# One encoder layer on one core: the gates' stores ahead of a large load, four reorderings, and the last tile pair's sums made by TensorE

## The reference

```python
def _swiglu(x, w_gate, w_up, w_down):
    return (jax.nn.silu(x @ w_gate) * (x @ w_up)) @ w_down

h = x
h = h + FFN_RES * _swiglu(_rmsnorm(h, ffn1_norm), ffn1_w_gate, ffn1_w_up, ffn1_w_down)   # FFN_RES = 0.5, D_FF = 2816
n = _rmsnorm(h, mix_norm)
z = n @ w_in                       # -> c_q 256 | c_kv 128 | k_rope 32 | u 512 | g_attn 1024 | g_ssm 1024
attn = ...                         # 8 heads, low-rank q and kv, rotary part of 32
y_ssm = ...                        # complex diagonal recurrence, forward and backward, plus ssm_d * u
glu = jax.nn.gelu(y_ssm) @ w_glu + b_glu
ssm_out = glu[..., :SSM_WIDTH] * jax.nn.sigmoid(glu[..., SSM_WIDTH:])
merged = (jax.nn.sigmoid(g_attn) * (attn @ w_o_attn) + jax.nn.sigmoid(g_ssm) * (ssm_out @ w_o_ssm))
h = h + merged @ w_out
h = h + FFN_RES * _swiglu(_rmsnorm(h, ffn2_norm), ffn2_w_gate, ffn2_w_up, ffn2_w_down)
out = _rmsnorm(h, final_norm)
```

## Time and profile before

| | |
|---|---|
| runs | 2243.97, 2243.58, 2242.82 us |
| median of the three | 2243.58 us |
| profiled execution | 2243.45 us |
| its span, first to last instruction | 2241.4 us |
| PE busy | 2140.1 us, 95% of the span |
| DVE, ACT, POOL busy | 66%, 41%, 27% |
| mean granted TensorE clock | 0.987 |

### The profile page before, as it was taken

How to read it: one execution, slowest core, us unless ns; L and a number is a source line. 1 busy time by engine, 2 the same in 40 slices (tenths; PEclk the granted TensorE clock), 3 DMA queues, 4 the chain that set the end, 5 groups by cost and what they waited for, 6 DMA issues and landing times. The chain is left out here.

```text
span 2241.4 us, 27668 instructions
## 1 busy us (share of the span) xinstructions
PE 2140.1 (95%) x10074; PEld 1770.1 (79%) x10074; DVE 1468.3 (66%) x2294; ACT 917.6 (41%) x1550; POOL 611.3 (27%) x510
## 2 busy tenths in 40 slices
PE   6999999999999998999999999899899999999997
PEld 4778888887887896787777887788688888887886
DVE  7787667657777527961557887554865656657777
ACT  5423323324445433124427778423523232324444
POOL 5336877740000012220002333100633333310000
PEclk9999999999999999999999999999999999999999
DMA  3434334349332545331440000274133232349333
GB/s 124 107 91 127 118 118 130 122 167 339 111 99 97 184 76 141 100 94 47 124 141 16 7 7 15 88 264 155 46 105 113 85 117 83 120 161 346 98 99 109
DMA packets 234583, 263.00 MB, mean 117 GB/s; under 512 B 34832, under 2 KB 169488, under 8 KB 233936
## 3 DMA queue, kind: packets, MB, share of 16 engines
q1 hardware_dynamic: 234448, 261.23, 36.7%
HBM read 184.60 MB, written 76.58 MB: 117 GB/s over the span
## 5 line engine op out<-in xcount | busy, mean ns | idle before, releaser
L48 PE MATMUL psum<-f_B_hi,f_A_hi 128*128 128x512 f32 x1232 | 487.5, 396 | 21.9 <-DVE f_A_lo L1048 10.1
L50 PE MATMUL psum<-f_B_hi,f_A_lo 128*128 128x512 f32 x1232 | 482.3, 392 | 0.0
L49 PE MATMUL psum<-f_B_lo,f_A_hi 128*128 128x512 f32 x1232 | 482.2, 391 | 0.0
L48 PEld LDWEIGHTS psum<-f_B_hi,f_A_hi 128*128 128x128 f32 x1232 | 232.9, 189 | 73.6 <-DVE f_A_lo L1048 17.1
L50 PEld LDWEIGHTS psum<-f_B_hi,f_A_lo 128*128 128x128 f32 x1232 | 232.8, 189 | 49.3
L49 PEld LDWEIGHTS psum<-f_B_lo,f_A_hi 128*128 128x128 f32 x1232 | 233.1, 189 | 47.3
L938 ACT CAST f_A_hi<-f_S 128x512 fp32r<-128x512 f32 x176 | 109.3, 622 | 347.0 <-PE psum L50 339.6
L48 PE MATMUL psum<-f_wd,f_hh 128*128 128x512 f32 x616 | 240.6, 391 | 3.6 <-DVE f_wd L1094 3.6
L49 PE MATMUL psum<-f_wd,f_hh 128*128 128x512 f32 x616 | 240.3, 390 | 0.0
L50 PE MATMUL psum<-f_wd,f_hh 128*128 128x512 f32 x616 | 240.2, 390 | 0.0
L1318 POOL TENSOR_TENSOR f_S<-f_raw 128x512 f32<-128x512 f32 x86 | 129.0, 1500 | 300.9 <-DVE f_A_lo L1048 280.3
(11 more groups left out here) (336 smaller groups left out, 4179.2 us busy)
## 6 DMA issues: line engine op xcount, KB each, us to landing
f_h_raw<-hidden SPq DMA_DIRECT2D x154, 256.0 KB, 2.7
hidden<-rows SPq DMA_DIRECT2D x44, 768.0 KB, 4.5
f_raw<-ffn_w_gate SPq DMA_DIRECT2D x44, 512.0 KB, 5.2
f_raw<-ffn_w_up SPq DMA_DIRECT2D x44, 512.0 KB, 5.0
f_wd_raw<-ffn_w_down SPq DMA_DIRECT2D x44, 512.0 KB, 9.2
rows<-x SPq DMA_DIRECT2D x16, 512.0 KB, 7.0
ga_raw<-w_in SPq DMA_DIRECT2D x16, 512.0 KB, 4.4
gates<-ga_sig SPq DMA_DIRECT2D x32, 256.0 KB, 2.4
```

The lines of the kernel that those rows point to most:

```text
L48: pe.matmul(out, lhs_hi, rhs_hi, start=first, stop=False, skip_group_check=go_on)
L49: pe.matmul(out, lhs_hi, rhs_lo, start=False, stop=False, skip_group_check=go_on)
L50: return pe.matmul(out, lhs_lo, rhs_hi, start=False, stop=last, skip_group_check=go_on)
```

## The change

Six things are changed; line numbers of the code before stand in brackets.

1. In both FFN fronts the sums of the last tile pair are no longer made by POOL and turned. `turn_last_sums` writes them into the banks as products of the normalised rows (stationary, plain f32) with the identity or with a new tile `minus` = -identity, which ACT makes once: 4 x (1 + 2 + 2 + 3 + 4) = 48 products of 128 columns in place of 20 transposes.
2. Between the last matrix and the units DVE's parts for unit 2 stand between the second and the third `pair_sum` (they stood behind the first weight difference).
3. In the last group of units each `final_row` stands one unit earlier. At the end of the second FFN `final_var(2)` stands ahead of `final_row(5)`, and the last row is scaled and stored in two halves.
4. The square of row 2 moves from the end of the first FFN to the start of the projection. There DVE makes the lo parts of turns 0 to 3 and `rp.low(0)` ahead of the norm's inverse root, and PE makes turn 4 behind the first product instead of ahead of it, so that each later turn moves back by one product.
5. In the SSM phase the load of `C_mat` is cut into four of 1024 KB, issued ahead of the stores of gates 2 to 5; the stores of gates 0 and 1 and the load for gate 4 come ahead of them.
6. In the mixer the two lo parts of keys move from n = 1 to n = 3 and n = 4.

```diff
     def act(self, act, rp):
         rest = slice(0, ST - self.AHEAD)
+        self.act_square(act, ST - self.AHEAD - 2)
         self.act_square(act, ST - self.AHEAD - 1)
...
-        dve.wait_ge(self.s_sq, 1)
+        dve.wait_ge(self.s_sq, 2)
         dve.tensor_scalar(st[:, 1, rest], st[:, 0, rest], 1.0 / D, EPS, ALU.mult, ALU.add).then_inc(self.s_var, 1)
-        self.dve_low(dve, 0)
+        for i in range(self.AHEAD):
+            self.dve_low(dve, i)
+        rp.low(dve, 0)
         dve.wait_ge(self.s_sqrt, 1)
...
-        self.dve_rows(dve, 4)
-        for i in range(1, self.AHEAD):
-            self.dve_low(dve, i)
+        self.dve_rows(dve, self.AHEAD)
         for i in range(self.AHEAD, ST):
-            rp.low(dve, i - self.AHEAD)
+            if i > self.AHEAD:
+                rp.low(dve, i - self.AHEAD)
...
+            act.mul(minus[:], ident[:], -1.0).then_inc(s_minus, 1)
             lows_high(1)
...
-                for m in range(QUAD - 1):
+                for m in range(QUAD - 2):
...
                     if p + 1 == PAIRS:
-                        for i in range(4):
-                            pair_sum(p, i)
+                        pair_sum(p, 0)
+                        pair_sum(p, 1)
+                        unit_low(2)
+                        pair_sum(p, 2)
+                        pair_sum(p, 3)
...
-                if v:
+                if v > 1:
                     unit_low(v + 1)
...
-                if closing and q == PRODUCTS - 1 and k >= 7:
-                    final_row(k - 7)
+                if closing and q == PRODUCTS - 1 and 6 <= k < 6 + QUAD:
+                    final_row(k - 6)
...
                 final_row(4)
+                final_var(2)
                 final_row(5)
-                final_var(2)
                 last.inverse(dve, 2, FGROUPS[2])
                 final_row(6)
-                final_row(7)
+                final_row(7, left)
+                final_row(7, right)
...
-            for i in range(QUAD):
+            for i in range(QUAD - 1):
                 combine(i)
...
+            def turn_last_sums():
+                m = QUAD - 1
+                lo_, hi_ = rows[:, m, :], rows[:, QUAD + m, :]
+                B11, B21, B12, B22 = lo_[:, 0:HALF], lo_[:, HALF:], hi_[:, 0:HALF], hi_[:, HALF:]
+                pe.wait_ge(s_minus, 1)
+                pe.wait_ge(s_xn, QUAD + m + 1 - ahead)
+                for i, parts in enumerate((((B22, 1),), ((B12, 1), (B11, -1)), ((B22, 1), (B12, -1)),
+                                           ((B22, 1), (B12, -1), (B11, 1)), ((B21, 1), (B22, -1), (B12, 1), (B11, -1)))):
+                    pe.wait_ge(s_blo, sum_turned(m - 1, i))
+                    for k in range(KH):
+                        sl = slice(k * P, (k + 1) * P)
+                        for a, (src, sign) in enumerate(parts):
+                            mm = pe.matmul(psum[:, SUM_BLOCKS[i], sl], src[:, sl], ident[:] if sign > 0 else minus[:], start=a == 0, stop=a == len(parts) - 1)
+                    mm.then_inc(s_tr, 1)
...
-            for i in range(norm.AHEAD + 1):
+            for i in range(norm.AHEAD):
                 norm.pe(pe, i)
             for n in range(rp.S):
                 if n == 0:
                     pe.wait_ge(norm.s_lo, norm.AHEAD)
                 rp.tiles(pe, n, ahead, rest[-1])
-                if norm.AHEAD + 1 + n < ST:
-                    norm.pe(pe, norm.AHEAD + 1 + n)
+                norm.pe(pe, norm.AHEAD + n)
...
-            sp.dma_start(C_mat[:], C_dram.rearrange("c p g x -> p c g x")).then_inc(s["c"], 16)
-            side.sync(sp)
+            for n in range(side.N):
+                if 4 <= n + 2 < side.N:
+                    side.gp.load(sp, n + 2)
+                if n == 2:
+                    sp.wait_ge(s["within"], NQ)
+                    sp.wait_ge(s["ud"], NQ)
+                if 2 <= n < 2 + C_PIECES:
+                    c, g0 = (n - 2) // 2, (n - 2) % 2 * GROUPS // 2
+                    g = slice(g0, g0 + GROUPS // 2)
+                    sp.dma_start(C_mat[:, c, g], C_dram[c][:, g]).then_inc(s["c"], 16)
+                side.store(sp, n)
...
-                if n == 1:
-                    for par in range(2):
-                        dve.wait_ge(s["kr_hi"], par + 1)
+                if n in (3, 4):
+                    par = n - 3
```

More of the change, by code:

```diff
@@ L729, in ffn_phase @@
         t1_of = lambda n: t1 if n else t1_first[:]
+        minus = at("minus", [P, P], F32, "ring", 6 * KB)
         dump = at("dump", [P, D], F32, "B_hi", 8 * KB)
@@ L763, in ffn_phase @@
         s_raw = [sem(f"raw_in{j}") for j in range(2)]
+        s_minus = sem("minus")
         s_sum, s_hi, s_lo, s_mm = map(sem, ("sum", "hi", "lo", "mm"))
@@ L885, in _ @@
             if finish:
-                for i, m in enumerate(FINAL):
+                for i, (m, cols) in enumerate([(m, slice(0, D)) for m in FINAL[:-1]] + [(FINAL[-1], left), (FINAL[-1], right)]):
                     sp.wait_ge(s_y, i + 1)
-                    sp.dma_start(finish[1][m * P:(m + 1) * P, :], rows[:, m, :]).then_inc(s_out, 16)
-                sp.wait_ge(s_out, 16 * ST)
+                    sp.dma_start(finish[1][m * P:(m + 1) * P, cols], rows[:, m, cols]).then_inc(s_out, 16)
+                sp.wait_ge(s_out, 16 * (ST + 1))
         @block.scalar
@@ L1227, in add_w_low, with final_row @@
                 into(low_right(i), u5[:, i, :], s_o12, 0, i)
-            def final_row(i):
+            def final_row(i, cols=slice(0, D)):
                 m = FINAL[i]
@@ L1232, in final_row @@
                     dve.wait_ge(s_store[i], 16)
-                dve.scalar_tensor_tensor(out=rows[:, m, :], in0=rows[:, m, :], scalar=stat[:, 3, i:i + 1], in1=fgain[:],
+                dve.scalar_tensor_tensor(out=rows[:, m, cols], in0=rows[:, m, cols], scalar=stat[:, 3, i:i + 1], in1=fgain[:, cols],
                                          op0=ALU.mult, op1=ALU.mult).then_inc(s_y, 1)
@@ L1419, in _ @@
                     first_product(*EARLY[m + 1])
-                turn_sums(m)
+                if m < QUAD - 1:
+                    turn_sums(m)
+                else:
+                    turn_last_sums()
             for j in range(2):
@@ L1602, in store @@
             sp.dma_start(self.gates[n * P:(n + 1) * P, half * HALF:(half + 1) * HALF], self.sig[:, half, :]).then_inc(self.out[half], 16)
-    def sync(self, sp):
-        for n in range(self.N):
-            if 4 <= n + 2 < self.N:
-                self.gp.load(sp, n + 2)
-            self.store(sp, n)
-        for half in range(2):
-            sp.wait_ge(self.out[half], 16 * self.N)
     def sigmoid(self, act, n):
@@ L1626 @@
 BLOCKS = 4
+C_PIECES = 4
 GATES_AFTER = (13, 14, None, 15)
@@ L1666, in _ @@
             side.gp.load(sp, 3)
-            sp.wait_ge(s["within"], NQ)
-            sp.wait_ge(s["ud"], NQ)
-            sp.dma_start(C_mat[:], C_dram.rearrange("c p g x -> p c g x")).then_inc(s["c"], 16)
-            side.sync(sp)
+            for n in range(side.N):
[9 more added lines that the diff above has]
+                side.store(sp, n)
+            for half in range(2):
+                sp.wait_ge(side.out[half], 16 * side.N)
         @block.tensor
@@ L1707, in _ @@
             pe.wait_ge(s["ec"], 4 * NQ)
-            pe.wait_ge(s["c"], 16)
+            pe.wait_ge(s["c"], 16 * C_PIECES)
             for b in range(BLOCKS):
@@ L2314, in _ @@
                     value(m)
-                if n == 1:
-                    for par in range(2):
-                        dve.wait_ge(s["kr_hi"], par + 1)
-                        dve.tensor_tensor(KT_lo[C, par, :], krT[C, :], KT_hi[C, par, :].bitcast(F32), ALU.subtract).then_inc(s["kr_lo"], 1)
+                if n in (3, 4):
+                    par = n - 3
+                    dve.wait_ge(s["kr_hi"], par + 1)
+                    dve.tensor_tensor(KT_lo[C, par, :], krT[C, :], KT_hi[C, par, :].bitcast(F32), ALU.subtract).then_inc(s["kr_lo"], 1)
             split(1)
```

## The result

The changed kernel takes 2259.26 us (median of 4 runs, 2258.62 to 2262.01) against 2243.77 for the kernel before: 1.0070 times, 95% interval 1.0058 to 1.0082. It is slower, as forecast, by 15.5 us and not by 9.2 (the forecast of 2252.8 against the earlier median of 2243.58). It lies 6.5 us above the forecast and 0.8 us above the range. The profiled execution of after took 2259.35 us, its span is 2257.6.

The account below looks back on a forecast made before the run. PE, busy 95% of the span, was taken as the bound. From 2243.45 us, terms of +4.2 at full clock and +5.1 for clock falls gave 2252.8, range 2246.5 to 2258.5.

Parts of the forecast that it names:

- the start of the units: Both FFNs: unit 2's parts ready 1.8 us sooner, gap of 0.9 before unit 3; -2.6 first FFN, -0.9 second.
- the clock: New gaps in fronts and projection: a fall of 1.7 us counted behind half of six, +5.1 in all.
- Fronts, +7.1 each: Both FFN fronts: 48 plain f32 products at 0.224 us replace 20 transposes; product q = 3 comes 7.1 us later.
- the rival with cheap products: FFN fronts: plain f32 products run near transpose speed, 0.109 us each; fronts +1.6 each, total 2240.1; chance 0.05.
- the one with 0.44 us a product: FFN fronts: a plain f32 product takes 0.44 us, each front +17.3, total 2273; chance 0.02.
- Projection: End of first FFN and projection: serial turns of 6.54 us instead of 3.30; first scaled product +9.5 us.
- Clock behind the fronts: Gaps behind both FFN fronts: half a clock fall of 1.7 us counted behind each, 2 x 0.5 x 1.7.
- a fall behind every gap: Fronts and projection: the clock falls behind each of six new or longer PE gaps, +10.2, total 2257.9; chance 0.14.
- SSM gates: SSM phase: stores ahead of the load remove PE's 9.1 us wait at gate 3 and 1.6 of half clock; -10.7.
- mixer: Mixer: moving two lo parts of keys removes a PE wait, -2.4, and a clock fall, -1.7; -4.1 in all.
- tail: End of the kernel: earlier evictions, 0.9 kept, and the halved last row's earlier store, 0.3 kept; -1.2.
- wait came back at gate 5: SSM gates: half the gates' gain is given back at gate 5, +5.3, total 2258.1; chance 0.06.

Follow-up runs that it names:

- the mended order: The changed kernel with the projection weights' hi and lo parts of product n + 1 made ahead of turn n + 4's parts on ACT and DVE: 2247.62 us.
- the single parts: The kernel before with one part of the change alone: fronts 2260.7 us, projection 2262.44, SSM gates 2232.41, mixer keys 2239.3.

## Why the prediction was wrong

Direction and main terms stood. The change was forecast 6.3 us too small (9.2 for 15.5), and the upper end of the range was 0.8 too low. The step that failed is the start of the units (2); the term that was mis-sized is the clock (3 and 4).

1. **Fronts, +7.1 each: right**, to 0.1 us, in both. The price was taken from the SSM's products and not from the transposes, and the rival with cheap products fell, as did the one with 0.44 us a product. Two runs that add and remove the part alone give 16.1 and 15.1, clock included. The prediction's bound for that rival, 0.13 us a product for a total as before, leaves out its own 1.7 for the clock; with it the bound is 0.145. Nothing hangs on it, since 0.222 was measured.
2. **Start of the units: the step that failed.** "Ahead of two sums and the difference they are ready 1.8 us sooner" is right, and so are the 0.9 ahead of unit 3 (0.72) and the saved clock fall. The step named what stands ahead of the moved instructions on DVE and forgot what stands behind. The two pair sums come 1.2 us later, SP waits for them with its stores, and a wait of 8.4 us for the landing of other stores stands between them and unit 12's load. That load had 1.7 us to spare; it came some 2 us later and PE wanted it 2.5 us sooner, against the kernel's own delay. The -2.6 came out as -0.1. SP's load at 535.79 and ACT's cast for unit 12 at 540.20, both in the trace of before, would have shown it.
3. **Projection: the mechanism right, the clock mis-sized.** The serial chain of 6.54 was measured as 6.43 and 6.51, the first product came 8.6 us after the phase's start (8.8 expected), and the mended order removed the three gaps. The clock was counted as half a fall behind each gap, 3.4; it was 6.2: three falls behind four gaps where two were counted, and one of them twice as long as the others. The forecast took 1.7 for every fall, though of the four falls in the earlier trace rows only two were 3.4 us long; that at 722.7 lasted 6.8 and that at 889.9 10.2, both with idle time of PE inside. Why one fall among the four gaps was long and one gap had none stays open.
4. **Clock behind the fronts: a fall in both**, 1.4 and 1.6, where half was counted. The case "a fall behind every gap" (chance 0.14) came nearest, though not as told: five of the six gaps had a fall, one of them a double one, and together they cost 9.2 of its 10.2. Its 2257.9 would have been 2260.4 with the units' 2.5. Against a fall the prediction had the 3.0 us at the second FFN; there too the clock fell in the run with the fronts undone.
5. **SSM gates, mixer, tail: right**, -10.8, -3.6 and -1.0 against -10.7, -4.1 and -1.2. No wait came back at gate 5. The tail was not run alone; its -1.0 is read from the trace, and its forecast was in part a guess (0.9 and 0.3 "kept").
6. **The range** joined the bounds of single terms, but held the units' start to be certain. The clock, 4.0 off in the forecast, was still inside its bound of 10.2; the units were not bounded. With that term bounded at no gain the upper end would have been 2261, and the measured time inside.

The misses in the table add up: 2.5 and 0.5 for the units, 4.0 for the clock, 0.7 for mixer and tail, less 1.0 for the projection, the phase start and the gates, makes 6.7 between the two sums.

## What to carry to other kernels

An edit that moves an instruction forward moves others back: follow those to the queue that waits for them, the DMA queue first, and look how much time its next urgent load has to spare. Where idle gaps of PE follow each other closely, give their clock falls a wide bound: the four gaps here were forecast at 3.4 us and cost 6.2, while the half clock throughout the stretch would have cost some 13, an estimate from the four periods of 3.3 us of work. Work given to the engine that bounds the kernel is paid in full, however much it frees elsewhere: 48 small products made each front 7 us longer, and what they took off PE was 20 transposes and half a microsecond's wait for POOL.

## What the hardware showed

The moments of the clock's falls differ from run to run of nearly the same program. The wait of 3.0 us at the second FFN's start had clock 1.00 behind it in the kernel before and fell in the run with the fronts undone. Behind the four gaps of the projection (2.9, 2.9, 2.9 and 2.4 us) the fall came after some and not after others. The medians of the single parts (+16.1, +17.8, -12.2, -5.3) differ by 1 to 3 us from their shares in the trace of the kernel after (+17.2, +14.8, -10.8, -3.6). That falls at other moments make this difference is likely and not shown. Transposes of f32 kept the granted clock at 2.4 GHz as products did: behind each of four gaps filled with nothing but transposes it was 1.00, in one trace.
